# DeltaNet layer: diagonal blocks packed for one transfer each way, decay rows loaded later, exponents of N formed in the recurrence

## What is computed

```python
g = jnp.cumsum(g.reshape(B, H, N, C), -1)
decay = jnp.exp(jnp.where(tril, g[..., :, None] - g[..., None, :], -jnp.inf))
A = jnp.where(strict, jnp.einsum('bhnid,bhnjd->bhnij', kb, k) * decay, 0.0)
rhs = jnp.concatenate([v * beta[..., None], kb * jnp.exp(g)[..., None]], -1)
sol = lax.linalg.triangular_solve(eye + A, rhs, left_side=True, lower=True, unit_diagonal=True)
...
v_new = u_n - jnp.einsum('bhcd,bhde->bhce', w_n, S)
o = jnp.einsum('bhcd,bhde->bhce', qd_n, S) + jnp.einsum('bhij,bhje->bhie', qk_n, v_new)
S = S * gl_n[..., None, None] + jnp.einsum('bhcd,bhce->bhde', kd_n, v_new)
```

## Time and profile before

| | us |
|---|---|
| median of 3 runs | 1129.16 |
| lowest and highest | 1126.41 and 1130.42 |
| the profiled execution | 1132.07 |
| its span, first to last instruction | 1130.3 |
| TensorE busy | 814.6 (72%) |
| VectorE, ScalarE, GpSimd busy | 418.0, 322.9, 280.6 |
| GpSimd idle ahead of L976, for DMA | 230.8 in 8 times |

### The profile page before, as it was taken

One profiled execution on the slowest core, in us unless ns is written; L12 is line 12 of the kernel. 1 busy time (PEld: TensorE's weight loads), 2 busy tenths in 40 slices (PEclk: granted clock), 3 DMA queues, 4 the chain that ended last, 5 costly groups with the idle time before them and its releaser, 6 DMA issues.

```text
span 1130.3 us, 14986 instructions
## 1 busy us (share of the span) xinstructions
PE 814.6 (72%) x5183; PEld 486.4 (43%) x5183; DVE 418.0 (37%) x1012; ACT 322.9 (29%) x724; POOL 280.6 (25%) x684
## 2 busy tenths in 40 slices
PE   5596658999983439284979689697836944999850
PEld 0253225555541023153656566566635423555430
DVE  0318431111112850252556366464644252111105
ACT  0121313222222222242345254452631021222112
POOL 0000002333321000043626336254360001333220
PEclk8588778999987659588889698888976975999985
DMA  9997299967894982562342513424100085999942
GB/s 345 363 393 298 112 375 358 331 217 282 314 352 146 378 249 75 185 179 37 95 86 53 123 39 94 91 50 122 38 5 6 1 350 207 356 364 350 376 135 111
DMA packets 119779, 227.23 MB, mean 201 GB/s; under 512 B 43421, under 2 KB 85733, under 8 KB 105255
## 3 DMA queue, kind: packets, MB, share of 16 engines
q1 hardware_dynamic: 107232, 198.66, 51.8%
q0 software_dynamic: 8224, 22.56, 6.2%
q10 hardware_dynamic: 4263, 5.21, 1.4%
HBM read 213.25 MB, written 17.33 MB: 204 GB/s over the span
## 4 chain that ended last, share of the span: by engine, by line
PE 34%; DMA 25%; POOL 14%; DVE 11%; issue 5%; SPq 5%; ACT 4%; ACTq 1%; DVEq 0%; POOLq 0%
PE banks L607 10%; DMA h_cols<-in_w_down_dram 7%; POOL arena L982 6%; POOL arena L980 6%; PE banks L619 5%; DMA weight_ring<-in_w_mod_dram 4%; DMA arena<-h_of_tokens,row_now 3%; DMA inverted_blocks<-arena 3%; PE banks L1000 3%; DMA arena<-blocks 3%; PE banks L1714 3%; PE banks L250 2%; SPq L964 2%; PE banks L587 2%; DMA blocks<-arena 2%
## 5 line engine op out<-in xcount | busy, mean ns | idle before, releaser
L1000 PE MATMUL banks<-h_cols,weight_ring 128*128 128x512 f32 (+1 forms) x384 | 166.3, 571 | 0.9 <-ACT modulation L273 0.7
L666 DVE TENSOR_TENSOR arena<-arena,banks 128x128 f32<-128x128 f32 x42 | 12.1, 289 | 235.2 <-ACT arena L635 235.2
L250 PE MATMUL banks<-weight_ring,c_cols 128*32 128x512 f32 x384 | 62.0, 747 | 47.4 <-DMA weight_ring<-in_w_mod_dram 47.1
L1000 PEld LDWEIGHTS banks<-h_cols,weight_ring 128*128 128x128 f32 x384 | 76.0, 215 | 44.0 <-issue 37.5
L702 POOL DMA_INDIRECT y_of_tokens<-arena,place_now x42 | 42.8, 1018 | 195.9 <-ACT arena L642 195.9
L982 POOL TENSOR_TENSOR arena<-arena 128x60 f32<-128x60 f32 (+10 forms) x240 | 78.8, 328 | 18.8
L607 PE MATMUL banks<-weight_ring,arena 128*64 128x256 f32 x640 | 78.8, 403 | 6.4 <-DMA weight_ring<-in_w_down_dram 4.0
L980 POOL TENSOR_TENSOR arena<-arena 128x60 f32<-128x60 f32 (+10 forms) x240 | 78.4, 327 | 18.8
L680 POOL DMA_INDIRECT arena<-h_of_tokens,row_now x50 | 46.3, 925 | 99.4 <-DVE place_of_slot L568 49.0
L630 ACT COPY arena<-arena 64x1024 f32<-64x1024 f32 x46 | 48.1, 1045 | 77.7 <-PE banks L587 57.0
L587 PE MATMUL banks<-const,arena 64*128 64x64 f32 x352 | 57.1, 285 | 12.9 <-ACT arena L630 12.9
(11 more groups left out here) (265 smaller groups left out, 1409.2 us busy)
## 6 DMA issues: line engine op xcount, KB each, us to landing
weight_ring<-in_w_mod_dram SPq DMA_DIRECT2D x48, 1024.0 KB, 12.1
weight_ring<-in_w_gate_dram SPq DMA_DIRECT2D x16, 1024.0 KB, 7.4
weight_ring<-in_w_up_dram SPq DMA_DIRECT2D x16, 1024.0 KB, 10.4
weight_ring<-in_w_down_dram SPq DMA_DIRECT2D x16, 1024.0 KB, 12.7
weight_ring<-in_dn_w_in_dram SPq DMA_DIRECT2D x32, 512.0 KB, 6.6
arena<-in_w_gate_dram SPq DMA_DIRECT2D x8, 1024.0 KB, 12.1
arena<-in_w_up_dram SPq DMA_DIRECT2D x8, 1024.0 KB, 14.4
arena<-in_w_down_dram SPq DMA_DIRECT2D x8, 1024.0 KB, 17.9
```

Of the source, the lines that this page charges most:

```text
L250: mm = pe.matmul(m.ps[j * COL:(j + 1) * COL, 0, :], m.c_cols[:, k, :], w[:, j, :], start=(k == 0), stop=(k == KD - 1))
L1000: mm = pe.matmul(bank(6 + j % 2)[:, 0:CTX + SEQ - n0], head_w[h % 2][:, j, k, :], m.hT[:, k, n0:CTX + SEQ], start=(k == 0), stop=(k == KD ...
```

## The change

- Two new tiles, N_diag and W_diag (128 x 8 x 32). VectorE copies diagonal blocks 0 and 1 of N side by side into N_diag behind N, ScalarE blocks 2 and 3 (`act_diagonal`, behind its squares of q). SyncE moves N_diag out in one transfer, M in in one (a source repeated four times), and the inverted blocks into W_diag in one.
- VectorE transposes from W_diag; ScalarE copies W_diag into W (`act_place_blocks`), ahead of its first joining copy. TensorE's second joining products wait for that. W in waits for the reads of W_diag of the head before instead of the end of its recurrence.
- On SyncE the decay rows of head x + 2 go behind M and U of head x + 1.
- Arguments of N of head x + 2 are formed on VectorE in the second and third step of recurrence x; q's taps in its first two steps (3 and 2 instead of 2, 2 and 1). ScalarE forms the exponents of head x + 2 behind the last step of recurrence x, ahead of its copy of that head's k projection; its silu of q comes one recurrence step earlier.
- On TensorE five of the eight steps of v's projection stand ahead of the keys and three behind. On ScalarE the squares of k stand ahead of the copy of v's projection (for all but the first head).
- The DRAM layouts and the counts of the semaphores follow.

```diff
-        n_dram = nc.dram_tensor("blocks", (NB, SYS, BLK, BLK), F32).ap()
+        n_dram = nc.dram_tensor("blocks", (SYS, NB, BLK, BLK), F32).ap()
...
         def sp_blocks_out(sp, h):
-            sp.wait_ge(s("n_mat"), 2 * (h + 1))
-            for k in range(NB):
-                r = slice(k * BLK, (k + 1) * BLK)
-                sp.dma_start(n_dram[k].rearrange("s r c -> r s c"), N[h % 2][r, :, r]).then_inc(s("n_out"), 16)
+            sp.wait_ge(s("n_mat"), 3 * (h + 1))
+            sp.wait_ge(s("k_length"), 6 * (h + 1))
+            sp.dma_start(n_dram.rearrange("s k r c -> (k r) s c"), N_diag).then_inc(s("n_out"), 16)
 
         def sp_blocks_in(sp, h):
-            sp.wait_ge(s("n_out"), 16 * NB * (h + 1))
-            for g in range(4):
-                sp.dma_start(M[g * BLK:(g + 1) * BLK, :, :], n_dram.rearrange("k s r c -> (k s) r c")).then_inc(s("m_in"), 16)
-            sp.dma_start(U, n_dram.rearrange("k s (q g) c -> g (k s) q c", g=4)).then_inc(s("m_in"), 16)
+            sp.wait_ge(s("n_out"), 16 * (h + 1))
+            sp.dma_start(M, n_dram.rearrange("s k r c -> (s k) (r c)").unsqueeze(0).to_broadcast([4, BLK, BLK * BLK])
+                         ).then_inc(s("m_in"), 16)
+            sp.dma_start(U, n_dram.rearrange("s k (q g) c -> g (s k) q c", g=4)).then_inc(s("m_in"), 16)
...
             sp.wait_ge(s("u_out"), 16 * (h + 1))
             if h >= 1:
-                sp.wait_ge(s("o_done"), h)
-            else:
-                sp.wait_ge(s("w_clear"), 2)
-            for k in range(NB):
-                r = slice(k * BLK, (k + 1) * BLK)
-                sp.dma_start(W[r, :, r], w_dram[k].rearrange("s r c -> r s c")).then_inc(s("w_base"), 16)
+                sp.wait_ge(s("v_base"), h)
+                sp.wait_ge(s("joined"), 11 * (h - 1) + 3)
+            sp.dma_start(W_diag, w_dram.rearrange("s k r c -> (k r) s c")).then_inc(s("w_base"), 16)
...
+            if h >= 1:
+                dve.wait_ge(s("n_out"), 16 * h)
+            dve.wait_ge(s("n_mat"), 3 * h + 2)
+            for k in (0, 1):
+                ins = dve.tensor_copy(N_diag[quarter(k), :, :], N[h % 2][quarter(k), :, quarter(k)])
+            ins.then_inc(s("n_mat"), 1)
+
+        def act_diagonal(act, h):
+            if h >= 1:
+                act.wait_ge(s("n_out"), 16 * h)
+            act.wait_ge(s("n_mat"), 3 * h + 2)
+            for k in (2, 3):
+                ins = act.copy(N_diag[quarter(k), :, :], N[h % 2][quarter(k), :, quarter(k)])
+            ins.then_inc(s("k_length"), 1)
...
-                ins = dve.transpose(V[r, :, r], W[r, :, r])
+                ins = dve.transpose(V[r, :, r], W_diag[r, :, :])
...
+        def act_place_blocks(act, h):
+            act.wait_ge(s("w_base"), 16 * (h + 1))
+            if h >= 1:
+                act.wait_ge(s("o_done"), h)
+            else:
+                act.wait_ge(s("w_clear"), 2)
+            for k in range(NB):
+                ins = act.copy(W[quarter(k), :, quarter(k)], W_diag[quarter(k), :, :])
+            ins.then_inc(s("joined"), 1)
...
             if closed(x):
                 sp_inverse_out(sp, x)
-            if closed(x) and x + 2 < HEADS:
-                sp_along(sp, x + 2)
-            if closed(x):
                 sp_inverse_in(sp, x)
             if made(x):
                 sp_blocks_out(sp, x + 1)
                 sp_blocks_in(sp, x + 1)
+            if closed(x) and x + 2 < HEADS:
+                sp_along(sp, x + 2)
+            if made(x):
                 sp.wait_ge(s("proj"), proj_made(x + 1, 2))
...
+        V_FIRST = 5
+
         def pe_step(pe, x):
             if made(x):
-                pe_project(pe, x + 1, 1)
+                pe_project(pe, x + 1, 1, 0, V_FIRST)
                 pe_keys(pe, x + 1)
+                pe_project(pe, x + 1, 1, V_FIRST, KD)
...
-            if made(x) and x >= 0:
-                act_exp_n(act, x + 1)
             if closed(x):
                 act_exp_q(act, x)
             if made(x):
                 act_conv(act, x + 1, 0)
+            if x >= 0 and made(x):
+                act_squares_k(act, x + 1)
+                act_pad(act, x + 1, 1)
+            if x < 0:
                 act_pad(act, x + 1, 1)
                 act_squares_k(act, x + 1)
-            if x < 0:
                 act_exp_n(act, x + 1)
             if closed(x):
                 act_squares_q(act, x)
+            if made(x):
+                act_diagonal(act, x + 1)
             if leaves(x):
                 act_squares_o(act, x - 1)
             act_roots(act, x)
             if closed(x):
+                act_place_blocks(act, x)
                 scaled(minus_p5(act, x, 0), -1.0)
...
                 if made(x):
                     act_values(act, x + 1, st)
-                    if st == TT - 1:
+                    if st == TT - 2:
                         act_conv(act, x + 1, 2)
+                if st == TT - 1 and x + 2 < HEADS:
+                    act_exp_n(act, x + 2)
...
-                if made(x) and st < 3:
-                    dve_conv(dve, x + 1, 2, 2 * st, min(2 * st + 2, TAPS))
-                if st == 3 and x + 2 < HEADS:
-                    dve_n_args(dve, x + 2)
+                if made(x) and st < 2:
+                    dve_conv(dve, x + 1, 2, 3 * st, min(3 * st + 3, TAPS))
+                if x + 2 < HEADS and st in (1, 2):
+                    dve_n_args(dve, x + 2, *((0, 3), (3, SYS))[st - 1])
```

More of the change, by code:

```diff
@@ L826, in build @@
         QK = [take(256, "p (t n) -> p t n", t=XT) for _ in range(2)]
+        N_diag = take(256, "p (s n) -> p s n", s=SYS)
+        W_diag = take(256, "p (s n) -> p s n", s=SYS)
         P5 = take(256, "p (s n) -> p s n", s=SYS)
@@ L974, in then @@
                 pool.wait_ge(s("block_step"), n[0])
-            pool.wait_ge(s("m_in"), 80 * (h + 1))
+            pool.wait_ge(s("m_in"), 32 * (h + 1))
             then(pool.tensor_tensor(U, U, v.strict_rows, ALU.mult))
@@ L996, in pe_project @@
                 if j == 2:
-                    pe.wait_ge(s("k_length"), 5 * (h + 1))
+                    pe.wait_ge(s("k_length"), 6 * h + 5)
             n0 = 0 if j < 2 else CTX
@@ L1087, in act_squares_k @@
                 act.wait_ge(s("lengths"), lengths_at(h - 1, 2))
-                act.wait_ge(s("k_length"), 5 * h)
+                act.wait_ge(s("k_length"), 6 * h)
             for t in range(TT):
@@ L1114, in act_roots @@
             if made(x):
-                act.wait_ge(s("k_length"), 5 * (x + 1) + TT)
+                act.wait_ge(s("k_length"), 6 * (x + 1) + TT)
                 act.activation(length[:, 0:4], ss_k, ACT.Sqrt, bias=L2_EPS).then_inc(s("root"), 1)
@@ L1122, in act_roots, with dve_n_args @@
                 act.activation(length[:, 6:8], ss_o, ACT.Sqrt, bias=L2_EPS, scale=1.0 / P).then_inc(s("root"), 1)
-        def dve_n_args(dve, h):
+        def dve_n_args(dve, h, u0=0, u1=SYS):
             dve.wait_ge(s(f"along{h % 2}"), 32 * (h // 2 + 1))
             if h >= 2:
-                dve.wait_ge(s("n_out"), 16 * NB * (h - 1))
+                dve.wait_ge(s("n_mat"), 3 * (h - 1))
+                dve.wait_ge(s("k_length"), 6 * (h - 1))
                 dve.wait_ge(s("join_mm"), 6 * (h - 2) + 4)
-            for d in DIRS:
-                for t in range(TT):
-                    dve.tensor_scalar(N[h % 2][:, d * TT + t, :], along[h % 2][:, d, t, :], col[:, h, d * TT + t:d * TT + t + 1],
-                                      0.0, ALU.add, ALU.min).then_inc(s("n_args"), 1)
+            for u in range(u0, u1):
+                d, t = divmod(u, TT)
+                dve.tensor_scalar(N[h % 2][:, u, :], along[h % 2][:, d, t, :], col[:, h, u:u + 1], 0.0, ALU.add, ALU.min
+                                  ).then_inc(s("n_args"), 1)
         def act_exp_n(act, h):
@@ L1163, in dve_n @@
         def dve_n(dve, h):
-            dve.wait_ge(s("k_length"), 5 * h + TT)
+            dve.wait_ge(s("k_length"), 6 * h + TT)
             dve.tensor_scalar(ss_eps, ss_k, L2_EPS, None, ALU.add).then_inc(s("lengths"), 1)
@@ L1237, in dve_turn_blocks @@
         def dve_turn_blocks(dve, h):
-            dve.wait_ge(s("w_base"), 16 * NB * (h + 1))
+            dve.wait_ge(s("w_base"), 16 * (h + 1))
             if h >= 1:
                 dve.wait_ge(s("o_done"), h)
+            else:
+                dve.wait_ge(s("w_clear"), 2)
             for k in range(NB):
                 r = quarter(k)
-                ins = dve.transpose(V[r, :, r], W[r, :, r])
+                ins = dve.transpose(V[r, :, r], W_diag[r, :, :])
             ins.then_inc(s("v_base"), 1)
@@ L1247, in pe_join32 @@
             pe.wait_ge(s("v_base"), h + 1)
-            pe.wait_ge(s("n_mat"), 2 * (h + 1))
+            pe.wait_ge(s("n_mat"), 3 * h + 2)
             if h >= 1:
@@ L1264, in pe_close32 @@
         def pe_close32(pe, h):
-            pe.wait_ge(s("joined"), 10 * h + 2)
-            pe.wait_ge(s("w_base"), 16 * NB * (h + 1))
+            pe.wait_ge(s("joined"), 11 * h + 3)
             for u in range(SYS):
```

(10 more changed lines are left out.)

5 lines of the change are left out of this document (3 added, 2 removed).

## The result

The changed kernel takes 1160.5 us (median of 4 runs, 1157.6 to 1161.4) against 1128.9 for the kernel before beside it: a ratio of 1.028 (95% interval 1.025 to 1.030), so slower by 32 us. The profiled execution took 1160.39 us, its span 1158.6, 28 more than before. The prediction was 1115 us, faster, with a range up to 1129.

What follows compares the result with a forecast made beforehand. Bound by a DMA and GpSimd loop with the engines' loop beside it; loops of 43.2, 43.8 and 44.25 us a head put the last inversion 15.7 earlier, less 1.45: -14.2 us, 1115 us, range 1103 to 1129.

Steps and rivals of the forecast that it cites:

- M and U: 0.45 + 4.7 = 5.15, at worst 6.45 as before: SyncE's loads before each inversion: M in one issue, then U landing, 5.15 us, at best 5.1.
- queue loop: DMA and GpSimd chain per head: inversion 26.6, N out 4.85, W in and N out 6.6, M and U 5.15: 43.2 us.
- the cover is 10 to 15 us: Decay rows issued some 4 us after the turn, first needed in the recurrence's second step: 10 to 15 us to spare.
- N out 4.85, W in 4.75: Single transfers of N's diagonal out and inverted blocks in, priced by U's measured landings: 4.85 and 4.75 us.
- Rival 2: W in and N out don't overlap, taking 9.6 us: loop 46.2 a head, 1127 us, within 0.3%; chance 0.13.
- last leg: Last head, U out to VectorE's turn of the inverted blocks: 8.15 us becomes 9.6, +1.45, as one W transfer lands later.
- T to R: T: VectorE's turn of inverted blocks; R: recurrence's end on TensorE; P: inversion's start. T to R taken as 26.3 us.
- two-head loop: Loop through both engines and DMA chain over two heads: 88.5 us, so 44.25 a head.
- engines' loop: VectorE and TensorE per head: 26.3 us turn to recurrence end, plus 17.5 until VectorE is ready: 43.8 us.
- Rival 4: M's broadcast may be cut into small pieces; even 10 us makes each of 8 heads 5 us longer: 1155; chance 0.03.
- Rival 3: TensorE's clock falls to 1.2 GHz after the new pause: 1163 us, a short drop 1121; chance of slower 0.10.
- Rival 1: N is not late, its copies ready 12.3 us after the recurrence; queue's 43.2 a head rules: 1106 us; chance 0.16.

Runs made afterwards that it cites:

- m4: Changed kernel with M fetched by four transfers again, all else as changed: 1118.5 us, ratio 0.990 to the kernel before.
- m4_along: m4 with the decay rows back ahead of the inverted blocks on SyncE's queue: 1131.8 us, ratio 1.001 to the kernel before.
- after_v8: Changed kernel, M still in one transfer, v's projection whole ahead of the keys and its copy ahead of k's squares: 1135.7 us, ratio 1.006.
- ginner_v8: ginner with v's projection whole ahead of the keys and its ScalarE copy ahead of the squares of k: 1085.7 us, ratio 0.960.
- m4_v8: m4 with v's projection whole ahead of the keys and its ScalarE copy ahead of the squares of k: 1092.9 us, ratio 0.968.
- ginner: Changed kernel with GpSimd's rows ordered (block, g): M one transfer with 32 outermost, U in and out in four transfers each: 1107.1 us, ratio 0.978.

## Why the prediction was wrong

**The step that failed** is a term of the sum: "M and U: 0.45 + 4.7 = 5.15, at worst 6.45 as before". It measured 11.4. I counted what M in one transfer saves in issues, 1.3 us, and let its data be "hidden by U's landing"; that one transfer could use fewer DMA engines than the four before it was not among my prices. Nor was M hidden before: the single packets of the kernel before have M's from 814.59 to 816.90 and U's from 816.76 to 819.44, one behind the other, so that whatever slows M moves U. In the changed kernel's third head M's run from 634.30 to 641.47 and U's from 640.77 to 643.88. The clue was in the trace of before: the slices of 813 to 821 us above hold M's data at 0.9 and U's at 0.3 of the engines, two kinds of transfer in one view. I put U's 4.8 us down to its pieces of 128 bytes, and so never asked what else set it. With the measured 11.4 the sum's queue loop would be 43.2 + 6.2 = 49.4 a head. That this is near the measured 50.1 is luck: its terms for N out and W in were too long, and what rules is not that loop but the one over the decay rows.

**Decay rows: "the cover is 10 to 15 us".** This cover was compared with nothing. Issue and landing had to be laid against it: in m4 the first half is issued at T + 3.5, the second 2.5 us later, and that one takes 12.0 to land. The rows are thus there at T + 18.0, when VectorE wants them at T + 17.6. In the changed kernel the issue grew to 9.3 us, and TensorE waited for 4.7 us in this head and 6.0 us in the one before it. The view of DMA of the kernel before, 617 to 645 us, has the landing (KB each, median us):

```profile
x_rows<-decay_rows SPq DMA_DIRECT2D x2, 256.0 KB, 10.2
```

I had not put it beside the cover. The sentence "if it were gone, the recurrence would wait" named what then happened. The gain of taking them away from ahead of W was right in kind, but smaller: some 2 us a head by m4_along, where the prediction has 3.6.

**N out 4.85, W in 4.75.** Too long by 2.5 us, for the same reason: I took U's row for them, but they run on more engines (N out 2.28 us in the chain, W in 2.39 in the last head). The fit of the Trainium skill ("DMA: Bandwidth & Descriptors", Anatomy of one DMA) that I weighed against the row, an estimated 2.3 us, was met for these two transfers and missed for U out, which takes 4.8. The mistake was the claim that "the row is of the very same kind of transfer". Rival 2 fell with it; and the last leg, +1.45 in the sum, was none: from P to T in the last head it is 31.4 us in m4, 32.0 before.

**The engines' part was right.** Timelines of VectorE and TensorE of the changed kernel, third head, R = 614.69:

```profile
614.74 4.53 PE L999 MATMUL banks<-h_cols,weight_ring 128*128 128x512 f32 x10
621.99 0.66 PE L1053 MATMUL banks<-const,arena 128*128 128x128 f32 x4 [2.73 <-ACT arena L1045]
...
623.38 2.74 PE L999 MATMUL banks<-h_cols,weight_ring 128*128 128x512 f32 x6
```

```profile
626.78 0.49 DVE L1037 TENSOR_SCALAR h_rows<-arena 128x512 f32<-128x512 f32 x1 [4.16 <-ACT arena L1017]
...
627.60 2.16 DVE L1174 SCALAR_TENSOR_TENSOR arena<-arena,banks 128x128 f32<-128x128 f32 x8
```

Keys at R + 7.3 (predicted 7.35), the pause 2.73 (2.9), N done at R + 15.1 (15.1), N out issued at R + 16.0 (16.0), the turn at R + 17.2 (17.5). T to R was 26.3 in the sum, 31.5 here with the wait, 25.5 in m4 (616.15 to 641.66). The sum's total is met by m4: 44.25 us a head predicted, 44.3 measured; its last inversion starts at 802.4, predicted 804.4; 1118.5 us, predicted 1115. So near a hit is in part luck. The 44.25 were those of the two-head loop, but in m4 the engines' loop rules: VectorE turns the third head's blocks at 616.15 and the fourth's at 660.49, without idle time before either (25.5 us to R, then 18.8), which the sum had at 43.8. In the two-head loop N out and W in were too long by 2.5 us each, M and U (6.6) too short by 1.4, and the waits for decay rows missing. What the prediction described is, in kind, the change with M left in four transfers.

**Rival 4** had the place and nearly the price: "even 10 would make each of 8 heads 5 us longer than forecast: 1155". But its cause, small pieces, was not the one (M still comes in 128 packets of 4 KB), it knew nothing of the decay rows, and "M's rows are 4 KB contiguous on both sides" was taken as enough to give it 0.03. The text had also said "wrong if M and U take over 6.5 us".

**Rival 3**, TensorE's clock, came in small. After the pause of 2.73 above the six matmuls of v took 2.74 us, at a granted clock of 1.00 (2.4 GHz); in the next head, after a pause of 2.99, they took 4.30, and the clock from 672.5 to 676.8 us was 0.64, a mean of its two levels:

```profile
670.98 0.66 PE L1053 MATMUL banks<-const,arena 128*128 128x128 f32 x4 [2.99 <-ACT arena L1045]
672.50 4.30 PE L999 MATMUL banks<-h_cols,weight_ring 128*128 128x512 f32 x6
```

From 676.8 us on it was 1.00 again. That is 1.6 us in such a head, as the "short drop" I priced at 1.8, not the 6 us that rival 3 needed.

**Rival 1** (N not late) is what after_v8, ginner_v8 and m4_v8 measure from the other side: N's lateness was real, and worth 3 to 3.7 us a head where nothing else ruled.

## What to carry to other kernels

Before several DMAs are made one, look at the outermost dimension of both sides of the new one, a repeat of the source included: here 4 instead of 32 outermost made the same 512 KB, with U behind it, nearly twice as long to arrive (11.4 us against 6.25; M's packets alone 7.0 against 1.85), and the share of busy DMA engines (0.9 against 0.2 to 0.3) tells it at once, in the trace of before too. When a load is moved later in a queue, lay its issue *and* its landing against the time at which it is used, and ask how long what now stands ahead of it takes: a slow transfer also makes the issue behind it slow. A duration taken over from another transfer holds only if shape and order of dimensions are the same, not only size and length of pieces.

## What the runs showed of the hardware that I had not expected

- The order of dimensions alone sets the pace of a transfer: M as (4, 32, 4 KB) at about 0.2 of the DMA engines, as (32, 4, 4 KB) at 0.9 (the slices of the changed kernel and of ginner). Out of the arena, in 128-byte pieces, 128 KB landed in 4.8 us with an outermost dimension of 4 and in 2.28 with 128.
- Issuing waits for what is queued: the two issues of decay rows take 1.15 to 2.20 us in ginner, where all that stands ahead of them has 32 or 128 outermost, 2.91 behind U out in the earlier trace rows, 3.53 behind M in four transfers with U, 9.28 and 10.21 behind M in one with U (third and second head).
- The decay rows, two transfers of 256 KB that repeat the same four rows of 512 bytes for all 128 partitions, take 11.8 us to land in the changed kernel and 12.0 in m4 (the second of the two), so whether M was slow or fast; the kernel before has 10.2 (median of the two). While they land in m4 and ginner the DMA engines are mostly at 0.1 to 0.3 of their time and near 45 GB/s. Why they are that slow was not tried.
- A pause of TensorE does not decide by its length alone what clock follows. In m4 a pause of 2.65 us ended at 606.23 and one of 2.65 at 648.88; TensorE had been busy for 3 us on end ahead of each pause, at a granted clock of 1.00. In windows behind them (length, busy us of PE, PEld, DVE, ACT, POOL, then the granted clock, DMA share, GB/s):

```profile
607.00:610.00 3.00, 3.00 (x13) 1.76 (x13) 0.38 (x2) 1.53 (x9) 0.00 (x0) 1.00 0.30 48
...
651.00:653.00 2.00, 2.00 (x4) 0.85 (x3) 0.00 (x0) 0.20 (x1) 0.00 (x0) 0.50 0.18 27
```

2.4 GHz behind the first, 1.2 GHz for some 2 us behind the second. What tells them apart stays open.
